# Attention units of two heads and one query tile, on both halves of TensorE's array, turned by transposes

## The chip, the cores and the metric

The kernel runs on one core of a Trainium2 chip. The metric is the device time of one execution in microseconds. Beside the runs that are timed there is one execution that the hardware profiler recorded; its rows are what is read here. The engines are TensorE (PE; its weight loads stand apart as PEld), VectorE (DVE), ScalarE (ACT), GpSimd (POOL) and SyncE (SP), which issues the weight DMAs. Engines run their own instruction lists in order and meet at semaphores.

## The reference, cut to what matters

Two transformer blocks, each of two layers, over 256 tokens of width 1024; everything is float32. Four attentions occur:

```python
# layer 0: 12 query heads of 64, 4 key/value heads; 256 context and 256 latent tokens
s = einsum('bkgqd,bksd->bkgqs', q, k) * 64 ** -0.5
p = softmax(s); o = einsum('bkgqs,bksd->bkgqd', p, v)
# context queries look at 256 keys, latent queries at 512
# layer 1: 6 heads with two 64-wide halves each, values 128 wide, 256 latent queries, 512 keys
p = softmax(einsum('bhiqd,bhisd->bhiqs', q, k) * 64 ** -0.5)
a = p[:, :, 0] - lam * p[:, :, 1]; o = einsum('bhqs,bhsd->bhqd', a, v)
# layers 2 and 3: cross attention, 4 heads of 64, 256 queries, 256 keys
```

Around them stand projections, normalizations, feed-forward layers (layers 0 and 1), an mLSTM (layer 2), an RG-LRU (layer 3), and an expert layer with 16384 experts (layers 2 and 3), which is most of the time.

## The kernel before, in words

The program is a list of stages (`STAGES`). Each engine runs its part of a stage after `enter`, which waits until the engines that take part in earlier stages have left them. So an attention stage (`attend0` to `attend3`) doesn't overlap the stage behind it: the stage behind begins when the last of TensorE, ScalarE and VectorE has left. SyncE is not in the stages: it streams all weights through a ring of 6 slots and is ahead as far as the ring lets it. No attention stage uses the ring; `attend0` also has GpSimd at `pool_windows` (22 us of its own), which attention doesn't wait for.

An attention stage is a row of units (`units_of`). In layers 0, 2 and 3 a unit is one head with two query tiles of 128 queries (`r` = 0, 1): 24 units in layer 0 (12 with 256 keys, then 12 with 512), 4 in each of layers 2 and 3 (256 keys). The head's 64 rows lie in the lower or the upper half of the partitions. In layer 1 a unit is one head with its two 64-wide halves and one query tile: 12 units of 512 keys ("diff" units).

What a unit takes, with the lines of the profile:

- TensorE `scores` (L822): two products, contraction over 64 rows, 128 queries by 256 or 512 keys, to two PSUM banks. Each float32 product is two MATMUL instructions.
- VectorE `maxima` (L1615, L1616): row maxima of both, times -1/8.
- ScalarE `exps` (L1344): two exponentials from PSUM to `probs`, each with its row sum.
- VectorE `diagonals` (L1622, L1626): reciprocals of the sums and two 128x128 diagonal matrices of them; in layer 1 the second times -lambda.
- TensorE `turn` (L838; L835 for diff units): product of each 128x128 piece of `probs` with its diagonal, which divides and turns it at once; for diff units the two halves add up in PSUM. To banks 4 and 5 (`pair`).
- VectorE `turned` (L1636): one copy of all of it to `probsT`.
- TensorE `heads` (L850): values (stationary, 64 columns; 128 in layer 1) with `probsT` (256 queries wide; 128 in layer 1), added over the key pieces.
- ScalarE `heads` (L1353): copy of the result to `mixed`.

The order is written out. TensorE: `scores(0)`, then for each i `scores(i+1)`, `heads(i-1)`, `turn(i)`. ScalarE: `exps(i+1)`, `heads(i-1)`. VectorE: `diagonals(i)`, `maxima(i+1)`, `turned(i)`, and in layer 3 `rglru_scans(i)` behind it. Scores, `probs` and `probsT` are double buffered, the turned banks are not.

Of the kernel before, what the change touches and what calls it, by code (L numbers as in the profile page):

```python
# [25 lines left out]
ALU = mybir.AluOpType  # L26
ACT = mybir.ActivationFunctionType
# [6 lines left out]
P = 128  # L34
D = 1024
T = 256
KD = D // P
DEPTH = 2
HD = 64
# [24 lines left out]
CTX, LAT = 0, 1  # L64
# [53 lines left out]
def stages_of(engine, before):  # L118
# [8 lines left out]


FEATURES, TOKENS = "features", "tokens"
PROJECT = {  # L130
    0: [(0, 8, 0, 2 * T, FEATURES, P), (8, 2, 0, 2 * T, TOKENS, P), (10, 2, 0, 2 * T, FEATURES, P)],
    1: [(18, 4, T, T, FEATURES, P), (0, 6, T, T, FEATURES, P), (6, 6, 0, 2 * T, FEATURES, P),
# [151 lines left out]
def program(nc, a, out):  # L284
    ctx = ExitStack()
    with ctx:
# [3 lines left out]
        def sem(name):  # L290
            return ctx.enter_context(nc.semaphore(name))
# [42 lines left out]
        def over(v, n):  # L334
# [18 lines left out]
        diag = part(WORK + 4096, 4, P)  # L353
# [52 lines left out]
        s_ready, m_ready, e_ready, d_ready, t_ready, pt_ready, o_ready, o_out = (sem(n) for n in (  # L406
            "scores_ready", "max_ready", "exp_ready", "diag_ready", "turned", "turned_out", "heads_ready", "heads_out"))
# [46 lines left out]
        def units_of(l):  # L454
            units = []
            if l == 0:
                for s in (CTX, LAT):
                    for n, head in enumerate(Q_ORDER):
                        j, half, kv = n // 2, n % 2, head // 3
                        assert half == kv % 2  # L460
                        rows = slice(half * HD, (half + 1) * HD)
                        units.append(dict(
                            nk=T if s == CTX else 2 * T, diff=False, rows=(half * HD, HD),
                            q=[proj[rows, j, s * T + r * P:s * T + (r + 1) * P] for r in range(2)],
                            k=[proj[rows, 6 + kv // 2, 0:T if s == CTX else 2 * T]] * 2,
                            v=lambda c, kv=kv: proj[:, 8 + kv // 2, c * P + (kv % 2) * HD:c * P + (kv % 2 + 1) * HD],
                            out=mixed[rows, j, s * T:(s + 1) * T]))
            elif l == 1:
                for h in range(6):
                    for t in range(2):  # L470
                        units.append(dict(
                            nk=2 * T, diff=True, rows=(0, P),
                            q=[proj[r * HD:(r + 1) * HD, h, t * P:(t + 1) * P] for r in range(2)],
                            k=[proj[r * HD:(r + 1) * HD, 6 + h, :] for r in range(2)],
                            v=lambda c, h=h: proj[:, 12 + h, c * P:(c + 1) * P],
                            out=mixed[:, h, t * P:(t + 1) * P]))
            else:
                for h in range(4):
                    j, half = h // 2, h % 2
                    rows = slice(half * HD, (half + 1) * HD)  # L480
                    units.append(dict(
                        nk=T, diff=False, rows=(half * HD, HD),
                        q=[proj[rows, 24 + j, r * P:(r + 1) * P] for r in range(2)],
                        k=[mem_k[rows, j, T:2 * T]] * 2,
                        v=lambda c, j=j, half=half: mem_v[:, j, T + c * P + half * HD:T + c * P + (half + 1) * HD],
                        out=mixed[rows, (6 if l == 2 else 8) + j, 0:T]))
# [147 lines left out]
        def _(pe):  # L634
# [176 lines left out]
            def attend(l):  # L811

                units = units_of(l)
                enter(pe, f"attend{l}")
                base = n_unit[0]

                def scores(i):
                    u = units[i]
                    if base + i >= 2:
                        pe.wait_ge(e_ready, base + i - 1)  # L820
                    for r in range(2):
                        last = mm(scores_at(i, u["nk"])[:, r, :], u["q"][r], u["k"][r], start=True, stop=True)  # L822
                    last.then_inc(s_ready, 1)

                def turn(i):
                    u = units[i]
                    pe.wait_ge(d_ready, base + i + 1)
                    if base + i:
                        pe.wait_ge(pt_ready, base + i)
                    for c in range(u["nk"] // P):  # L830
                        for r in range(2):
                            e = probs[:, i % 2, r, c * P:(c + 1) * P]
                            dg = diag[:, 2 * (i % 2) + r, :]
                            if u["diff"]:
                                last = mm(pair[:, 0, c * P:(c + 1) * P], e, dg, start=(r == 0), stop=(r == 1))  # L835
                            else:
                                at = (c % 2) * T + r * P
                                last = mm(pair[:, c // 2, at:at + P], e, dg, start=True, stop=True)  # L838
                    last.then_inc(t_ready, 1)

                def heads(i):
                    u = units[i]
                    pe.wait_ge(pt_ready, base + i + 1)
                    if base + i >= 2:
                        pe.wait_ge(o_out, base + i - 1)
                    nq = P if u["diff"] else 2 * P
                    lo, m = u["rows"]
                    chunks = u["nk"] // P
                    for c in range(chunks):
                        last = mm(single[lo:lo + m, i % 2, 0:nq], u["v"](c), probsT[:, i % 2, c * nq:(c + 1) * nq],  # L850
                                  start=(c == 0), stop=(c == chunks - 1))
# [12 lines left out]
                leave()  # L864
# [326 lines left out]
        def _(act):  # L1191
# [136 lines left out]
            def attend(l):  # L1328
# [9 lines left out]
                def exps(i):  # L1338
# [7 lines left out]
                                 accum_out=cols[:, 16 + b + r:17 + b + r])  # L1346
                    last.then_inc(e_ready, 1)

                def heads(i):
                    u = units[i]  # L1350
                    act.wait_ge(o_ready, base + i + 1)
                    lo, m = u["rows"]
                    f(u["out"], single[lo:lo + m, i % 2, 0:P if u["diff"] else 2 * P], ACT.Copy).then_inc(o_out, 1)  # L1353
# [163 lines left out]
        def _(dve):  # L1517
# [89 lines left out]
            def attend(l):  # L1607
# [8 lines left out]
                    v.tensor_scalar(cols[:, 8 + b:10 + b], cols[:, b:b + 2], -HD ** -0.5, None,  # L1616
                                    ALU.mult).then_inc(m_ready, 1)

                def diagonals(i):
                    b = 4 * (i % 2)  # L1620
                    dve.wait_ge(e_ready, base + i + 1)
                    chain(v.reciprocal(cols[:, 24 + b:26 + b], cols[:, 16 + b:18 + b]))  # L1622
                    for r in range(2):
                        second = neg_lam[:, 0:1] if units[i]["diff"] and r else None
                        op = (ALU.mult, ALU.mult) if second is not None else (ALU.mult,)
                        last = v.tensor_scalar(diag[:, 2 * (i % 2) + r, :], const("ident"),  # L1626
                                               cols[:, 24 + b + r:25 + b + r], second, *op)
                    last.then_inc(d_ready, 1)

                def turned(i):  # L1630
                    u = units[i]
                    dve.wait_ge(t_ready, base + i + 1)
                    if base + i >= 2:
                        dve.wait_ge(o_ready, base + i - 1)
                    n = u["nk"] * (1 if u["diff"] else 2)
                    v.tensor_copy(probsT[:, i % 2, 0:n], ps[:, 4:6, :].rearrange("p b n -> p (b n)")[:, 0:n])\  # L1636
                        .then_inc(pt_ready, 1)
# [12 lines left out]

# [625 lines left out]
```

## Time and profile before

| what | value |
|---|---|
| median of 3 runs | 3855.55 us (3855.47 to 3856.93) |
| the profiled execution | 3852.96 us, its span 3851.1 us |
| mean granted TensorE clock | 0.903 |
| PE busy | 91% of the span |
| stage attend0 (158.0 to 276.4) | 118.4 us |
| stage attend1 (948.2 to 1003.3) | 55.1 us |
| stage attend2 (1464.3 to 1492.0) | 27.7 us |
| stage attend3 (2698.5 to 2727.5) | 29.0 us |

The busy time of an engine counts what it ran; the row of a timeline gives start, duration, engine, line, operation, operands, the number of merged instructions, and in brackets how long the engine sat idle before and for whom. The granted clock is 1.0 where TensorE ran at 2.4 GHz and 0.5 where it ran at 1.2 GHz.

### The profile page before, as it was taken

To read this page: it belongs to the slowest core of one execution; us is meant where nothing else is said; L and a number is where in the kernel's file an instruction comes from. 1 tells how busy PE (TensorE), PEld (TensorE's weight loads), DVE (VectorE), ACT (ScalarE), POOL (GpSimd) and SP (SyncE) were. 2 spreads that over 40 slices of the span, in tenths; PEclk is the share of its full clock that TensorE was granted. 3 is DMA by queue.
4 is the path that set the end of the run, shared out by engine and by line. 5 is a ranking of instruction groups with operands and counts; after the bars stand their busy time and mean duration, and the time that the engine had idled before them with its cause. 6 is when DMAs were issued, how large, how long until landed. Compare 5 with 4: busy or idle time off the path is not lost.

```text
span 3851.1 us, 59762 instructions
## 1 busy us (share of the span) xinstructions
PE 3505.1 (91%) x21992; PEld 3056.0 (79%) x21992; DVE 2161.2 (56%) x3899; ACT 1226.0 (32%) x1840; POOL 93.5 (2%) x135
## 2 busy tenths in 40 slices
PE   7998998999889996679999999998758999999998
PEld 3567988967689765579999989986658899899997
DVE  2444545543455223866666666664396666666665
ACT  1223424421244212013444144443201444324444
POOL 0200000000000000200000000000020000000000
PEclk9999999999999987858999599999885899959999
DMA  7304545552145321203555045543120355504553
GB/s 268 135 10 172 185 169 186 185 197 88 44 148 185 127 77 44 88 0 118 187 185 186 21 158 185 186 160 120 60 77 0 136 185 186 188 2 174 186 187 128
DMA packets 140460, 512.94 MB, mean 133 GB/s; under 512 B 15904, under 2 KB 15904, under 8 KB 139584
## 3 DMA queue, kind: packets, MB, share of 16 engines
q1 hardware_dynamic: 139712, 507.48, 37.6%
q0 software_dynamic: 640, 4.00, 0.3%
q8 instruction: 71, 1.16, 0.1%
q14 instruction: 37, 0.30, 0.0%
HBM read 510.37 MB, written 1.05 MB: 133 GB/s over the span
## 4 chain that ended last, share of the span: by engine, by line
PE 85%; DVE 9%; ACT 2%; issue 1%; DMA 1%; PEld 1%; DVEq 0%; ACTq 0%; POOL 0%; PEldq 0%; SPq 0%; POOLq 0%
PE ps L878 29%; PE ps L936 22%; PE ps L1119 10%; PE ps L869 4%; PE ps L755 4%; PE ps L713 3%; PE ps L758 1%; PE ps L850 1%; PE ps L822 1%; PE ps L838 1%; PE ps L1081 1%; PE ps L907 1%; PE ps L901 1%; DVE arena L1530 1%; PE ps L718 1%
## 5 line engine op out<-in xcount | busy, mean ns | idle before, releaser
L1728 DVE TENSOR_TENSOR w_split<-ring,w_split 128x1024 fp32r<-128x1024 f32 x710 | 869.3, 1226 | 689.5 <-ACT w_split L1405 666.2
L878 PEld LDWEIGHTS ps<-x_split,w_split 128*128 128x128 f32 x9312 | 1170.5, 194 | 72.9 <-issue 48.0
L878 PE MATMUL ps<-x_split,w_split 128*128 128x256 f32 x9312 | 1179.7, 285 | 46.1 <-DVE w_split L1728 46.1
L1405 ACT ACTIVATE w_split<-ring 128x1024 fp32r<-128x1024 f32 x710 | 751.0, 1060 | 1126.8 <-PE ps L878 677.3
L936 PE MATMUL ps<-w_split,h_split 128*128 128x512 f32 x3864 | 934.3, 391 | 0.0
L936 PEld LDWEIGHTS ps<-w_split,h_split 128*128 128x128 f32 x3864 | 706.0, 188 | 133.7
L1119 PE MATMUL ps<-arena 128*128 128x64 bf16 x3072 | 373.6, 302 | 16.3 <-DVE arena L2019 16.3
L1119 PEld LDWEIGHTS ps<-arena 128*128 128x128 bf16 x3072 | 372.7, 146 | 17.6 <-issue 17.6
L1436 ACT ACTIVATE arena<-ps 128x512 f32 x128 | 77.1, 602 | 328.2 <-PE ps L1119 328.2
L1749 DVE TENSOR_TENSOR x<-x,arena 128x256 f32<-128x256 f32 x256 | 158.3, 618 | 16.6 <-ACT x L1411 16.6
L869 PE MATMUL ps<-arena,ring 128*128 128x256 f32 (+1 forms) x672 | 150.1, 386 | 9.2 <-DVEq L1524 7.1
L755 PE MATMUL ps<-arena,ring 128*128 128x512 f32 (+1 forms) x416 | 153.2, 522 | 4.8 <-ACTq L1197 4.8
L869 PEld LDWEIGHTS ps<-arena,ring 128*128 128x128 f32 (+1 forms) x672 | 130.1, 194 | 29.8 <-issue 10.7
L713 PE MATMUL ps<-x,ring 128*128 128x256 f32 (+1 forms) x608 | 133.6, 382 | 6.3 <-ACTq L1197 6.3
L1081 PE MATMUL ps<-x,ring 128*128 128x256 f32 x512 | 122.3, 395 | 18.7 <-DVEq L1524 18.7
L755 PEld LDWEIGHTS ps<-arena,ring 128*128 128x128 f32 x416 | 80.5, 195 | 67.7 <-issue 62.6
L713 PEld LDWEIGHTS ps<-x,ring 128*128 128x128 f32 (+1 forms) x608 | 109.2, 180 | 30.1 <-issue 7.1
L2015 DVE TENSOR_TENSOR arena<-arena 128x512 bf16<-128x512 bf16 x128 | 54.5, 425 | 134.4 <-PE ps L1119 124.7
L1081 PEld LDWEIGHTS ps<-x,ring 128*128 128x128 f32 x512 | 99.7, 200 | 33.0 <-issue 19.4
L1530 DVE RECIPROCAL arena<-arena 128x256 f32<-128x256 f32 (+2 forms) x26 | 63.1, 2429 | 107.1 <-ACT arena L1308 107.1
L2019 DVE TENSOR_TENSOR arena<-arena 128x1536 bf16<-128x1536 bf16 x128 | 121.8, 952 | 0.0
L1739 DVE TENSOR_TENSOR h_split<-x,h_split 128x256 fp32r<-128x256 f32 x256 | 109.1, 426 | 8.7
(258 smaller groups left out, 2423.6 us busy)
## 6 DMA issues: line engine op xcount, KB each, us to landing
ring<-in_peer_u SPq DMA_DIRECT2D x256, 512.0 KB, 3.2
ring<-in_peer_v SPq DMA_DIRECT2D x256, 512.0 KB, 3.2
ring<-in_ffn_in SPq DMA_DIRECT2D x132, 512.0 KB, 3.2
ring<-in_ada SPq DMA_DIRECT2D x96, 512.0 KB, 4.5
ring<-in_ffn_out SPq DMA_DIRECT2D x66, 512.0 KB, 3.2
ring<-in_pq SPq DMA_DIRECT2D x32, 512.0 KB, 3.2
ring<-in_ml_in SPq DMA_DIRECT2D x26, 512.0 KB, 3.2
ring<-in_cd_in SPq DMA_DIRECT2D x22, 512.0 KB, 3.4
```

The costliest lines, as they stand in the source:

```text
L713: last = mm(pair[0:width, par, 0:nt], w[:, k, :], src[:, k, t0:t0 + nt], start=(k == 0), stop=(k == KD - 1))
L755: last = mm(pair[:, n % 2, 0:nt], w[:, k, :], hT[:, k, t0:t0 + nt], start=(k == 0), stop=(k == KD - 1))
L869: last = mm(wide[:, m, :], ring[0:rows, blk[0], m * P:(m + 1) * P], rhs, start=(first and m % 2 == 0), stop=final, skip_group_check=True)
L878: last = mm(dst, w_split[:, w, wp, at:at + P], rhs[rp], start=(first and i == 0), stop=(final and i == 2), skip_group_check=shared)
L936: last = mm(ps[:, 2 * r + c, :], h_split[:, ph, hp, r * P:(r + 1) * P], w_split[:, b[3], wp, c * 512:(c + 1) * 512], start=(first and i == ...
L1081: last = mm(pair[:, m % 2, 0:T], ring[:, b[0], k * P:(k + 1) * P], x[:, LAT, k, :], start=(k == 0), stop=(k == KD - 1))
L1119: last = mm(single[:, b, u * HALF:(u + 1) * HALF], hot_i[:, b, :, u], hot_w[:, b, c, :, u], start=(c == 0), stop=(c == 2))
L1405: f(w_split[:, w, 0, :], ring[:, slot, :], ACT.Copy).then_inc(w_high, 1)
L1728: v.tensor_tensor(w_split[:, w, 1, :], ring[:, slot, :], w_split[:, w, 0, :].bitcast(F32), ALU.subtract).then_inc(w_low, 1)
L1739: v.tensor_tensor(h_split[:, ph, 1, :], raw[:, ph, :], h_split[:, ph, 0, :].bitcast(F32), ALU.subtract).then_inc(hid_ready, 1)
L1749: return v.tensor_tensor(coef[:, ph, :], gelu[:, ph, :], g, ALU.mult)
L2019: v.tensor_tensor(hot_w[:, b], hot_j[:, b].unsqueeze(1).to_broadcast([P, 3, HALF, GROUP]), weight3[:, :, at].unsqueeze(2).to_broadcast([P, ...
```

## The change

Units of layers 0, 2 and 3 become two heads (the lower and upper half of the partitions) with one query tile; their number stays the same. The diagonals go: VectorE's `divided` scales `probs` in place, and `turn` becomes one transpose for each 128x128 piece. For diff units `divided` forms p1/s1 - lambda p2/s2 first, so half as many pieces are turned. The copy of the turned pieces is parted: VectorE the first head, ScalarE the second; ScalarE alone for diff units. VectorE's order becomes `maxima(i+1)`, `divided(i)`, `turned(i-1)`; ScalarE's `exps(i+1)`, `turned(i-1)`, `heads(i-2)`. TensorE's order stays `scores(i+1)`, `heads(i-1)`, `turn(i)`.

```diff
+HALVES = [slice(0, HD), slice(HD, P)]
...
-                    for n, head in enumerate(Q_ORDER):
...
+                    for j in range(6):
+                        kv = Q_ORDER[2 * j] // 3 // 2
...
+                        for r in range(2):
+                            at = s * T + r * P
+                            units.append(dict(
+                                nk=nk, diff=False, q=[proj[rows, j, at:at + P] for rows in HALVES],
+                                k=[proj[rows, 6 + kv, 0:nk] for rows in HALVES],
+                                v=lambda c, half, kv=kv: proj[:, 8 + kv, c * P + half * HD:c * P + (half + 1) * HD],
+                                out=mixed[:, j, at:at + P]))
...
                 def turn(i):
                     u = units[i]
                     pe.wait_ge(d_ready, base + i + 1)
                     if base + i:
-                        pe.wait_ge(pt_ready, base + i)
-                    for c in range(u["nk"] // P):
-                        for r in range(2):
-                            e = probs[:, i % 2, r, c * P:(c + 1) * P]
-                            dg = diag[:, 2 * (i % 2) + r, :]
...
+                        pe.wait_ge(pt_second, base + i)
+                    if not u["diff"] and firsts + i:
+                        pe.wait_ge(pt_first, firsts + i)
+                    for half in range(1 if u["diff"] else 2):
+                        for c in range(u["nk"] // P):
+                            last = nc.tensor.transpose(pair[:, half, c * P:(c + 1) * P],
+                                                       probs[:, i % 2, half, c * P:(c + 1) * P], const("ident"))
                     last.then_inc(t_ready, 1)
                 def heads(i):
                     u = units[i]
-                    pe.wait_ge(pt_ready, base + i + 1)
+                    pe.wait_ge(pt_second, base + i + 1)
+                    if not u["diff"]:
+                        pe.wait_ge(pt_first, firsts + i + 1)
...
                     for c in range(chunks):
+                        for half in range(1 if u["diff"] else 2):
+                            rows = slice(0, P) if u["diff"] else HALVES[half]
+                            last = mm(single[rows, i % 2, 0:P], u["v"](c, half),
+                                      probsT[:, i % 2, half * 512 + c * P:half * 512 + (c + 1) * P],
+                                      start=(c == 0), stop=(c == chunks - 1))
...
+                def turned(i):
+                    u = units[i]
+                    act.wait_ge(t_ready, base + i + 1)
+                    if base + i >= 2:
+                        act.wait_ge(o_ready, base + i - 1)
+                    half = 0 if u["diff"] else 1
+                    f(probsT[:, i % 2, half * 512:half * 512 + u["nk"]], pair[:, half, 0:u["nk"]], ACT.Copy)\
+                        .then_inc(pt_second, 1)
...
                 exps(0)
                 for i in range(n):
                     if i + 1 < n:
                         exps(i + 1)
                     if i:
-                        heads(i - 1)
+                        turned(i - 1)
+                    if i >= 2:
+                        heads(i - 2)
+                turned(n - 1)
+                heads(n - 2)
                 heads(n - 1)
...
-                def diagonals(i):
+                def divided(i):
                     b = 4 * (i % 2)
                     dve.wait_ge(e_ready, base + i + 1)
                     chain(v.reciprocal(cols[:, 24 + b:26 + b], cols[:, 16 + b:18 + b]))
...
+                    one, two = (probs[:, i % 2, half, 0:units[i]["nk"]] for half in range(2))
+                    if units[i]["diff"]:
+                        v.tensor_scalar(cols[:, 26 + b:27 + b], cols[:, 25 + b:26 + b], neg_lam[:, 0:1], None, ALU.mult)
+                        chain(v.tensor_scalar(one, one, cols[:, 24 + b:25 + b], None, ALU.mult))
+                        last = v.scalar_tensor_tensor(one, two, cols[:, 26 + b:27 + b], one, ALU.mult, ALU.add)
+                    else:
+                        v.tensor_scalar(one, one, cols[:, 24 + b:25 + b], None, ALU.mult)
+                        last = v.tensor_scalar(two, two, cols[:, 25 + b:26 + b], None, ALU.mult)
                     last.then_inc(d_ready, 1)
...
                 maxima(0)
                 for i in range(n):
-                    diagonals(i)
                     if i + 1 < n:
                         maxima(i + 1)
-                    turned(i)
+                    divided(i)
+                    if i and not units[i - 1]["diff"]:
+                        turned(i - 1)
                     if l == 3:
                         rglru_scans(i)
+                if not units[n - 1]["diff"]:
+                    turned(n - 1)
```

## Rows read from the trace of the kernel before

**Rows 1.** The page's chain that ended last, shares of the span by engine.
```profile
PE 85%; DVE 9%; ACT 2%; issue 1%; DMA 1%; PEld 1%; DVEq 0%; ACTq 0%; POOL 0%; PEldq 0%; SPq 0%; POOLq 0%
```

**Rows 2.** Stretches: length, busy PE, PEld, DVE, ACT, POOL; granted clock, DMA share, GB/s.
```profile
158.00:276.40 118.40, 110.29 (x528) 69.78 (x528) 65.74 (x144) 38.77 (x121) 21.83 (x21) 0.96 0.02 5
948.20:1003.30 55.10, 49.06 (x336) 38.48 (x336) 31.49 (x72) 23.26 (x64) 0.00 (x0) 0.97 0.03 11
1464.30:1492.00 27.70, 21.03 (x64) 13.46 (x64) 8.43 (x24) 6.83 (x21) 0.00 (x0) 0.53 0.00 0
2698.50:2727.50 29.00, 18.98 (x64) 12.09 (x64) 17.47 (x34) 6.76 (x21) 0.00 (x0) 0.65 0.00 1
...
1018.00:1022.00 4.00, 2.47 (x6) 2.05 (x7) 2.47 (x3) 0.00 (x0) 0.00 (x0) 0.50 0.02 4
1022.00:1026.00 4.00, 4.00 (x19) 3.49 (x18) 0.00 (x0) 0.00 (x0) 0.00 (x0) 0.94 0.10 18
```

**Rows 3.** Timeline (start, duration, then what), attend0, units of 256 keys.
```profile
163.93 2.08 PE L838 MATMUL ps<-arena 128*128 128x128 f32 x8 [4.80 <-DVE arena L1626]
...
184.09 0.47 ACT L1344 ACTIVATE arena<-ps,cols 128x256 f32<-128x256 f32 x1 [1.34 <-DVE cols L1616]
...
185.00 0.37 ACT L1353 ACTIVATE arena<-ps 64x256 f32<-64x256 f32 x1
```

**Rows 4.** Timeline, attend0, units of 512 keys.
```profile
202.80 1.23 DVE L1615 TENSOR_REDUCE cols<-ps 128x2 f32<-128x1024 f32 x1 [0.63 <-PE ps L822]
...
204.26 0.69 ACT L1344 ACTIVATE arena<-ps,cols 128x512 f32<-128x512 f32 x1 [2.98 <-DVE cols L1616]
...
205.60 0.37 ACT L1353 ACTIVATE arena<-ps 64x256 f32<-64x256 f32 x1
...
215.45 1.98 PE L822 MATMUL ps<-arena 64*128 64x512 f32 x4
...
217.36 1.94 PE L850 MATMUL ps<-arena 128*64 128x256 f32 x8
...
219.23 2.05 PE L838 MATMUL ps<-arena 128*128 128x128 f32 x16
...
221.21 1.98 PE L822 MATMUL ps<-arena 64*128 64x512 f32 x4
```

**Rows 5.** Timeline, attend1, the first two diff units.
```profile
948.22 1.99 PE L822 MATMUL ps<-arena 64*128 64x512 f32 x8 [0.77 <-ACTq L1197]
...
949.49 1.23 DVE L1615 TENSOR_REDUCE cols<-ps 128x2 f32<-128x1024 f32 x1 [12.26 <-PE ps L822]
...
954.28 3.63 PE L835 MATMUL ps<-arena 128*128 128x128 f32 x16 [4.07 <-DVE arena L1626]
```

**Rows 6.** Timeline, attend2, first units, the clock at 0.5.
```profile
1471.03 2.08 PE L838 MATMUL ps<-arena 128*128 128x128 f32 x8 [4.55 <-DVE arena L1626]
...
1473.04 2.07 PE L822 MATMUL ps<-arena 64*128 64x256 f32 x4
...
1475.15 0.69 DVE L1615 TENSOR_REDUCE cols<-ps 128x2 f32<-128x512 f32 x1 [0.72 <-PE ps L822]
...
1476.08 0.47 ACT L1344 ACTIVATE arena<-ps,cols 128x256 f32<-128x256 f32 x1 [3.24 <-DVE cols L1616]
```

**Rows 7.** Timeline of TensorE: transposes behind a hidden stage; products on four 32-column groups.
```profile
521.39 1.97 PE L965 MATMUL ps<-consts,arena 128*128 128x128 f32 x16 [0.69 <-ACT arena L1426]
...
89.72 1.50 PE L652 MATMUL ps<-ring,cond_wide 128*32 128x256 f32 x24
```

**Rows 8.** Groups by line (busy us, mean ns of one): copies, a scaling; and a scan pair in attend3.
```profile
L1436 ACT ACTIVATE arena<-ps 128x512 f32 x128 | 77.1, 602 | 328.2 <-PE ps L1119 328.2
L1411 ACT ACTIVATE x<-ps 128x256 f32<-128x256 f32 x256 | 94.3, 368 | 20.9 <-PE ps L878 20.9
L1668 DVE TENSOR_SCALAR res<-x 128x2048 f32<-128x2048 f32 x6 | 7.3, 1224 | 1.7 <-ACTq L1197 1.1 <-DVEq L1524 0.6
...
2709.93 1.27 DVE L1904 TENSOR_TENSOR_SCAN arena<-arena 96x256 f32<-96x256 f32 x2
```

More of the change, by code:

```diff
@@ L352, in program @@
         probsT = part(WORK + 2048, 2, 1024)
-        diag = part(WORK + 4096, 4, P)
         h2 = part(0, KD, T)
@@ L405, in program @@
             "squared", "mean_ready", "normed", "partner_ready", "roped"))
-        s_ready, m_ready, e_ready, d_ready, t_ready, pt_ready, o_ready, o_out = (sem(n) for n in (
-            "scores_ready", "max_ready", "exp_ready", "diag_ready", "turned", "turned_out", "heads_ready", "heads_out"))
+        s_ready, m_ready, e_ready, d_ready, t_ready, pt_first, pt_second, o_ready, o_out = (sem(n) for n in (
+            "scores_ready", "max_ready", "exp_ready", "divided", "turned", "first_head_kept", "second_head_kept", "heads_ready",
+            "heads_out"))
         sum_ready = sem("sum_ready")
@@ L457, in units_of @@
                 for s in (CTX, LAT):
-                    for n, head in enumerate(Q_ORDER):
[L459 to L467, printed above, removed]
+                    nk = T if s == CTX else 2 * T
@@ new lines, in units_of @@
+                    for j in range(6):
+                        kv = Q_ORDER[2 * j] // 3 // 2
+                        assert [Q_ORDER[2 * j + half] // 3 for half in range(2)] == [2 * kv, 2 * kv + 1]
+                        for r in range(2):
[5 more added lines that the diff above has]
+                                out=mixed[:, j, at:at + P]))
@@ L468, in units_of @@
             elif l == 1:
                 for h in range(6):
-                    for t in range(2):
+                    for r in range(2):
                         units.append(dict(
[L472 to L476, printed above, removed]
-            else:
[L478 to L486, printed above, removed]
@@ L487, in units_of @@
-            return units
+                            nk=2 * T, diff=True, q=[proj[rows, h, r * P:(r + 1) * P] for rows in HALVES],
+                            k=[proj[rows, 6 + h, :] for rows in HALVES],
+                            v=lambda c, half, h=h: proj[:, 12 + h, c * P:(c + 1) * P],
+                            out=mixed[:, h, r * P:(r + 1) * P]))
+            else:
+                for j in range(2):
+                    for r in range(2):
+                        units.append(dict(
+                            nk=T, diff=False, q=[proj[rows, 24 + j, r * P:(r + 1) * P] for rows in HALVES],
+                            k=[mem_k[rows, j, T:2 * T] for rows in HALVES],
+                            v=lambda c, half, j=j: mem_v[:, j, T + c * P + half * HD:T + c * P + (half + 1) * HD],
+                            out=mixed[:, (6 if l == 2 else 8) + j, r * P:(r + 1) * P]))
@@ L489, in scores_at, with first_heads @@
+            return units
+        def first_heads(l):
+            return 24 if l == 1 else sum(len(units_of(m)) for m in range(l) if m != 1)
         def scores_at(i, nk):
@@ L814, in attend @@
                 enter(pe, f"attend{l}")
-                base = n_unit[0]
+                base, firsts = n_unit[0], first_heads(l)
                 def scores(i):
@@ L828, in turn @@
                     if base + i:
-                        pe.wait_ge(pt_ready, base + i)
-                    for c in range(u["nk"] // P):
-                        for r in range(2):
-                            e = probs[:, i % 2, r, c * P:(c + 1) * P]
-                            dg = diag[:, 2 * (i % 2) + r, :]
[L834 to L838, printed above, removed]
+                        pe.wait_ge(pt_second, base + i)
[5 more added lines that the diff above has]
+                                                       probs[:, i % 2, half, c * P:(c + 1) * P], const("ident"))
                     last.then_inc(t_ready, 1)
@@ L842, in heads @@
                     u = units[i]
-                    pe.wait_ge(pt_ready, base + i + 1)
+                    pe.wait_ge(pt_second, base + i + 1)
+                    if not u["diff"]:
+                        pe.wait_ge(pt_first, firsts + i + 1)
                     if base + i >= 2:
                         pe.wait_ge(o_out, base + i - 1)
-                    nq = P if u["diff"] else 2 * P
-                    lo, m = u["rows"]
                     chunks = u["nk"] // P
                     for c in range(chunks):
-                        last = mm(single[lo:lo + m, i % 2, 0:nq], u["v"](c), probsT[:, i % 2, c * nq:(c + 1) * nq],
-                                  start=(c == 0), stop=(c == chunks - 1))
+                        for half in range(1 if u["diff"] else 2):
[3 more added lines that the diff above has]
+                                      start=(c == 0), stop=(c == chunks - 1))
                     last.then_inc(o_ready, 1)
@@ L1347, in exps @@
                     last.then_inc(e_ready, 1)
+                def turned(i):
[6 more added lines that the diff above has]
+                        .then_inc(pt_second, 1)
                 def heads(i):
-                    u = units[i]
                     act.wait_ge(o_ready, base + i + 1)
-                    lo, m = u["rows"]
-                    f(u["out"], single[lo:lo + m, i % 2, 0:P if u["diff"] else 2 * P], ACT.Copy).then_inc(o_out, 1)
+                    f(units[i]["out"], single[:, i % 2, 0:P], ACT.Copy).then_inc(o_out, 1)
                 n = len(units)
@@ L1622, in diagonals @@
                     chain(v.reciprocal(cols[:, 24 + b:26 + b], cols[:, 16 + b:18 + b]))
[L1623 to L1627, printed above, removed]
+                    one, two = (probs[:, i % 2, half, 0:units[i]["nk"]] for half in range(2))
[6 more added lines that the diff above has]
+                        last = v.tensor_scalar(two, two, cols[:, 25 + b:26 + b], None, ALU.mult)
                     last.then_inc(d_ready, 1)
@@ L1634, in turned @@
                         dve.wait_ge(o_ready, base + i - 1)
-                    n = u["nk"] * (1 if u["diff"] else 2)
-                    v.tensor_copy(probsT[:, i % 2, 0:n], ps[:, 4:6, :].rearrange("p b n -> p (b n)")[:, 0:n])\
-                        .then_inc(pt_ready, 1)
+                    v.tensor_copy(probsT[:, i % 2, 0:u["nk"]], pair[:, 0, 0:u["nk"]]).then_inc(pt_first, 1)
                 n = len(units)
```

## The prediction

> **What bounds the kernel now.** I read the chain of waits first: the reader sees TensorE's products on 85% of it [rows 1], so what counts is how long TensorE is kept. Then the stretches of the four attention stages [rows 2]: together 118.4 + 55.1 + 27.7 + 29.0 = 230.2 us, 6% of the span, and nothing of another stage beside them, so a change of their length goes into the total in full. Then the timeline inside a stage. In a unit of 512 keys TensorE goes from scores (215.45) to heads (217.36) to turn (219.23) to the next scores (221.21) and has no idle time in brackets: 5.76 us a unit, all TensorE [rows 4]. The stretches say the same: PE busy 110.3 of 118.4 and 49.1 of 55.1. The order before lets VectorE and ScalarE work beside that. So before, these stages are bound by TensorE, at a granted clock of 0.96 and 0.97; attend2 and attend3 ran mostly at 1.2 GHz (0.53 and 0.65) [rows 2].
>
> **What the new order makes of it.** TensorE's list at step i is still scores(i+1), heads(i-1), turn(i). heads(i-1) now waits for ScalarE's copy of unit i-1, and that copy stands in ScalarE's list behind exps(i+1), which waits for VectorE's maxima(i+1), which wait for scores(i+1), issued by TensorE just before. So the whole step is one ring: scores(i+1), maxima(i+1), exps(i+1), copy(i-1), heads(i-1), turn(i), and only then scores(i+2). Nothing in it lies beside anything else. VectorE's own branch is shorter: after maxima(i+1) it has divided(i) and the copy of the first head. A scaling of 2048 columns takes 1.22 us [rows 8], so 512 take some 0.3; two of them with the reciprocal 0.9, the copy of 512 columns some 0.7, together 1.6 us, against exps and copy on ScalarE, 1.9 us. For diff units the second pass has two inputs; even at 0.7 us the diff division ends at 1.7 and has no copy behind it. This branch costs nothing; if it were 0.5 us longer, 0.2 us a step would show.
>
> **The terms of a step**, at 2.4 GHz first:
> - Scores. In layer 1 the two products already lie on both halves, and the timeline shows them side by side: 8 instructions of 512 columns in 1.99 us, where 4 of one half take 1.98 [rows 4, 5]. From their start to the start of the maxima: 1.27 us for 512 keys [rows 5]; for 256 keys half of the streaming goes (0.43), 0.84. At 1.2 GHz 4 serial instructions of 256 columns take 1473.04 to 1475.15, 2.11 us; two pairs side by side of 512 columns stream as long, 2.11, and of 256 columns 0.85 less, 1.26 [rows 6].
> - Maxima until exps start: 202.80 to 204.26, 1.46 us for 512 keys [rows 4]; 1475.15 to 1476.08, 0.93 for 256 [rows 6].
> - Both exps until ScalarE's next operation: 204.26 to 205.60, 1.34 [rows 4]; 184.09 to 185.00, 0.91 [rows 3].
> - Copy by ScalarE: 0.60 for 512 columns, 0.37 for 256 [rows 8], and 0.06 to hand on (the maxima start 0.04 behind the products' end, rows 6).
> - Heads. New are column halves side by side. The nearest row has four 32-column groups: 24 instructions of 256 columns in 1.50 us, six groups of four, so one group each (1.50 - 0.38)/5 = 0.22 us, as if it were one instruction [rows 7]. With 128 columns that is 0.11 for a pair: 4 pairs for 256 keys, 8 for 512, 8 full instructions in a diff unit. With 0.15 for the change of the tile: 0.59, 1.03, 0.9. At 1.2 GHz 1.04, 1.9, 1.8.
> - Turn. 16 transposes take 1.97 us, (1.97 - 0.27)/15 = 0.11 each, one instruction each [rows 7], where a product with a diagonal needs two (16 in 2.05 for 8 pieces, rows 4). So 4, 8, and 4 (diff) transposes and 0.2 until the next scores: 0.64, 1.07, 0.64; at 1.2 GHz 1.1, 1.96, 1.1.
>
> The Trainium skill, "TensorE: Matmul & The Clock Gate", section "Terms", says that the transpose mode is four times faster for FP32; the row shows twice against two-instruction diagonal products. By that rule the turns would be half as long again, and the sum below some 20 us smaller.
>
> Sums of a step at 2.4 GHz: 256 keys 0.84 + 0.93 + 0.91 + 0.43 + 0.59 + 0.64 = 4.3 us; 512 keys 1.27 + 1.46 + 1.34 + 0.66 + 1.03 + 1.07 = 6.8; diff 1.27 + 1.46 + 1.34 + 0.66 + 0.9 + 0.64 = 6.3. At 1.2 GHz: 1.26 + 0.93 + 0.91 + 0.43 + 1.04 + 1.1 = 5.7; 2.11 + 1.46 + 1.34 + 0.66 + 1.9 + 1.96 = 9.4; diff 2.11 + 1.46 + 1.34 + 0.66 + 1.8 + 1.1 = 8.5.
>
> **Which clock.** In both large stages TensorE waits 4.8 and 4.1 us for the first exps and then starts its turn at 1.2 GHz: 8 instructions in 2.08 us, 16 in 3.63 [rows 3, 5]. Before, it was then packed without a gap and came back to 2.4 GHz. In attend2 it was busy 21.0 of 27.7 us and stayed at 0.53 [rows 2]. In the new ring it works 3.2 of 5.7, 6.0 of 9.4, 5.0 of 8.5 us at the low level, less densely than in that stretch. I take it that the clock stays at 1.2 GHz through all four stages; that is my choice, and the other end is a rival. Of the transposes, the Trainium skill says ("TensorE: Matmul & The Clock Gate", Part 4) that they don't count as activity for the gate; no row here shows that, and it would only make the low level surer.
>
> **The sum.** attend0: the first turn starts at 163.9 [rows 3], with divided on 256 columns in place of 128 at 164.1, and ends its step at 165.2. Ten steps of 5.7 to 222.4; two mixed ones of 7.5 and 8.4 to 238.3; ten of 9.4 to 332.3; the last (no scores or exps left: copy, heads, turn, copy, heads, output) 0.75 + 1.9 + 1.96 + 0.75 + 1.9 + 0.5 = 7.8, to 340.1. Before 276.4: +63.7. attend1: first turn at 954.3 [rows 5] plus 0.9 for the longer division, its step ends 956.3; ten steps of 8.5 to 1041.3, end 6.7, 1048.0; before 1003.3: +44.7. attend2: first turn 1471.1, step ends 1472.2 [rows 6], two steps of 5.7 to 1483.6, end 4.8, 1488.4; before 1492.0: -3.6. attend3 the same shape, but after divided(0) VectorE has its scans before maxima(2) (a pair 1.27 us [rows 8]), and in the last step they stand ahead of its last copy: -2. Behind attend0, attend2 and attend3 a dense product stage now starts at 1.2 GHz. Such a start is seen behind attend1: 0.50 until 1022, 0.94 in the next 4 us [rows 2], TensorE starting at 1019.5; half of 2.7 us is lost: 3 x 1.4 = +4. Bounds 0 and 10 for the three. SyncE, the ring and the DMAs take nothing: no weights are used in these stages. Sum: 63.7 + 44.7 - 3.6 - 2 + 4 = +107 us on the profiled execution's 3853.0: 3960. The median of the runs stands 2.6 above that execution, so 3962.
>
> Unknown terms: column halves (below: none of the other direction; above: weight loads one after the other, a rival), the hand-on (0 to 0.2 us in 5 places of 36 steps: -10 to +20).
>
> **Rivals.**
> 1. The clock returns to 2.4 GHz, or does so for part of the stages. For: before, it came back in both large stages (0.96 and 0.97 over all), and the change makes the array fuller in scores and heads. Against: the gaps above. All of it: attend0 165.2 + 5.7 + 9 x 4.3 + 5.8 + 6.2 + 10 x 6.8 + 4.9 = 294.5 (+18), attend1 956.3 + 10 x 6.3 + 4.8 = 1024.1 (+21), the small stages -5.6: +34, 3889. In part: 3889 to 3940.
> 2. The ring isn't closed: ScalarE's copy gets by without the new exps, and the engines overlap. Then each step is its busiest engine: TensorE some 3.1 us for 512 keys (0.85 + 0.2 + 1.03 + 1.07) against 5.76, 2.0 against 3.15 for 256 keys (VectorE: 0.69 + 0.2 + 0.2 + 0.4 + 0.4), 2.9 against 3.93 for diff units (VectorE): 12 x (2.66 + 1.15 + 1.0) = -58, with the small stages -6: 3792, faster. It decides only if TensorE reaches heads(i-1) without waiting for exps(i+1). For it speaks that TensorE's own work falls by 40%; against it the two written orders.
> 3. The change doesn't do what it says in the heads: the loads of the two column halves come one after the other. Then 4 or 8 more loads a step at up to 0.23 us (1.2 GHz): +0.8 and +1.8 us, 11 x 0.8 + 12 x 1.8 = +30: 3992. Against: the four-group row.
>
> **Chances.** Forecast 0.73 (its own range 3940 to 3985); rival 1 0.17; rival 2 0.04; rival 3 0.05; a result within 0.2% (8 us, about what a measurement of this kernel tells from no change) 0.01. The range 3888 to 3988 reaches from rival 1 at its full size nearly to rival 3. Faster 0.04, same 0.01, slower 0.95.
>
> **What would show it.** In the profile after: a steady unit of 512 keys with scores, maxima, exps, ScalarE's copy, heads, turn one after another and TensorE idle before heads with ScalarE's copy as releaser, about 3.5 us; steps of 5.7, 9.4, 8.5 us; a granted clock near 0.5 in attend0 and attend1; transposes of 0.11 us (0.22 at the low level); the scans of attend3 unchanged. A step shorter than 5.76 us for 512 keys, or TensorE idle for VectorE instead, makes the ring wrong; steps near 6.8 make the clock wrong.

## Result, and the profile after

| | time, us |
|---|---|
| before | 3856.24 median (3855.47 to 3857.29, 4 runs) |
| after | 3942.39 median (3938.67 to 3946.68, 4 runs) |
| ratio | 1.0223, 95% interval 1.021 to 1.0236: slower |
| forecast | 3962 (3888 to 3988) |
| profiled execution after | 3946.68, span 3944.9, clock 0.88 |

The four attention stages after, as stretches (length, busy PE, PEld, DVE, ACT, POOL, granted clock, DMA share, GB/s); they answer to [rows 2]:

```profile
158.80:333.70 174.90, 98.59 (x529) 62.81 (x529) 63.63 (x144) 44.29 (x145) 21.51 (x21) 0.65 0.01 4
1004.90:1101.50 96.60, 54.78 (x192) 35.82 (x192) 33.91 (x73) 29.11 (x76) 0.00 (x0) 0.62 0.02 6
1561.60:1584.60 23.00, 13.17 (x65) 8.16 (x65) 7.79 (x24) 7.36 (x25) 0.00 (x0) 0.50 0.00 0
2794.30:2819.40 25.10, 13.17 (x65) 8.14 (x65) 16.76 (x34) 7.35 (x25) 0.00 (x0) 0.50 0.00 0
```

The stages took 118.4, 55.1, 27.7 and 29.0 us before and 174.9, 96.6, 23.0 and 25.1 after: +56.5, +41.5, -4.7, -3.9, together +89.4 of the 93.8 us by which the profiled spans differ. PE is busy 98.6 of 174.9 us where it was busy 110.3 of 118.4, and the clock went from 0.96 and 0.97 to 0.65 and 0.62.

One whole step of 512 keys with the clock high throughout, from the timeline of the changed kernel; it answers to [rows 4]. L825 are the scores, L1629 the maxima, L1347 the exps, L1636 starts the division, L1652 and L1358 are VectorE's and ScalarE's copies of the turned pieces, L852 is heads, L837 the turn:

```profile
294.25 1.13 PE L825 MATMUL ps<-arena 64*128 64x512 f32 x4
295.43 1.23 DVE L1629 TENSOR_REDUCE cols<-ps 128x2 f32<-128x1024 f32 x1 [5.00 <-PE ps L825]
...
296.76 0.16 DVE L1636 RECIPROCAL cols<-cols 128x2 f32<-128x2 f32 x1
296.89 0.69 ACT L1347 ACTIVATE arena<-ps,cols 128x512 f32<-128x512 f32 x1 [5.92 <-DVE cols L1630]
...
297.75 0.69 DVE L1652 COPY arena<-ps 128x512 f32<-128x512 f32 x1
298.23 0.59 ACT L1358 ACTIVATE arena<-ps 128x512 f32<-128x512 f32 x1
...
298.88 1.09 PE L852 MATMUL ps<-arena 128*64 128x128 f32 x16 [3.50 <-ACT arena L1358]
299.90 1.09 PE L837 MATMUL ps<-consts,arena 128*128 128x128 f32 x8
300.93 1.13 PE L825 MATMUL ps<-arena 64*128 64x512 f32 x4
```

These rows show the ring. From the scores it is 1.18 us to the maxima, 1.46 to the exps, 1.34 to ScalarE's copy, 0.65 to heads (TensorE idle for 3.50 us, ended by that copy), 1.02 to the turn and 1.03 to the next scores: 6.68 us. VectorE's copy ended at 298.44, 0.4 us before ScalarE's. All other full steps of 512 keys were longer, 8.42 to 9.12 us, with the clock low in part of them. A step of 256 keys, all at 1.2 GHz, answers to [rows 6]:

```profile
192.93 1.23 PE L825 MATMUL ps<-arena 64*128 64x256 f32 x4
194.21 0.69 DVE L1629 TENSOR_REDUCE cols<-ps 128x2 f32<-128x512 f32 x1 [3.70 <-PE ps L825]
...
195.14 0.47 ACT L1347 ACTIVATE arena<-ps,cols 128x256 f32<-128x256 f32 x1 [4.18 <-DVE cols L1630]
...
196.05 0.38 ACT L1358 ACTIVATE arena<-ps 128x256 f32<-128x256 f32 x1
...
196.49 1.12 PE L852 MATMUL ps<-arena 128*64 128x128 f32 x8 [2.33 <-ACT arena L1358]
197.54 1.12 PE L837 MATMUL ps<-consts,arena 128*128 128x128 f32 x4
198.59 1.22 PE L825 MATMUL ps<-arena 64*128 64x256 f32 x4
```

The waits of heads over the whole execution (who for whom, total us, times, longest), in the kernel before and then in the changed one:

```profile
PE ps L850 <- DVE arena L1636: 7.3, 8, 1.3
...
PE ps L852 <- ACT arena L1358: 110.2, 41, 3.5
```

### The profile page after: what moved, and what is told of

It is laid out like the page before. It is cut to its first block, busy times and chain, and to the rows that moved or that the text cites. A ratio compares the mean times of both kernels' runs of the same rounds, so it can differ in the third digit from the quotient of the medians.

```text
span 3944.9 us, 59550 instructions
## 1 busy us (share of the span) xinstructions
PE 3489.8 (88%) x21848; PEld 3041.3 (77%) x21848; DVE 2160.1 (55%) x3899; ACT 1238.6 (31%) x1884; POOL 93.1 (2%) x135
## 3 DMA queue, kind: packets, MB, share of 16 engines
HBM read 510.37 MB, written 1.05 MB: 130 GB/s over the span
## 4 chain that ended last, share of the span: by engine, by line
PE 83%; DVE 9%; ACT 3%; issue 1%; DMA 1%; PEld 1%; DVEq 0%; ACTq 0%; POOL 0%; PEldq 0%; SPq 0%; POOLq 0%
PE ps L881 28%; PE ps L939 22%; PE ps L1122 9%; PE ps L872 4%; PE ps L758 4%; PE ps L716 3%; PE ps L852 2%; PE ps L761 1%; PE ps L825 1%; PE ps L837 1%; DVE cols L1629 1%; PE ps L1084 1%; PE ps L910 1%; PE ps L904 1%; ACT arena L1347 1%
## 5 line engine op out<-in xcount | busy, mean ns | idle before, releaser
L852 PEld LDWEIGHTS ps<-arena 128*64 128x64 f32 (+1 forms) x448 | 53.4, 237 | 159.7 <-ACT arena L1358 152.9
L852 PE MATMUL ps<-arena 128*64 128x128 f32 (+1 forms) x448 | 69.2, 421 | 120.0 <-ACT arena L1358 110.2
L1629 DVE TENSOR_REDUCE cols<-ps 128x2 f32<-128x1024 f32 (+1 forms) x44 | 43.4, 986 | 175.0 <-PE ps L825 175.0
```

The costliest lines, as they stand in the source:

```text
L852: last = mm(single[rows, i % 2, 0:P], u["v"](c, half), probsT[:, i % 2, half * 512 + c * P:half * 512 + (c + 1) * P], start=(c == 0), stop ...
L1629: chain(v.tensor_reduce(cols[:, b:b + 2], scores_at(i, units[i]["nk"]), AX_X, ALU.max))
```

## Experiments

All edits are to the changed kernel. Times are medians of 4 runs; the kernel before had 3853.8 us in the first batch (copy-first, ScalarE only, filled, shape only) and 3857.5 in the second (VectorE only, best of both, products, first wait only). Ratios are to the kernel before in the same batch. Stage lengths are stretches of the profiled execution, from the stage's first instruction to the first of the next stage.

**1. Copies first, on both engines.**

```diff
 # ScalarE
-                    if i + 1 < n:
-                        exps(i + 1)
                     if i:
                         turned(i - 1)
+                    if i + 1 < n:
+                        exps(i + 1)
 # VectorE
-                    if i + 1 < n:
-                        maxima(i + 1)
-                    divided(i)
                     if i and not units[i - 1]["diff"]:
                         turned(i - 1)
+                    divided(i)
+                    if i + 1 < n:
+                        maxima(i + 1)
```

> The changed kernel with two order edits: ScalarE copies unit i-1 before the exps of unit i+1; VectorE does the copy of unit i-1, then divided(i), then maxima(i+1). Theory 1 (the closed ring: heads(i-1) waits for work that starts only with scores(i+1)) expects that TensorE reaches heads(i-1) straight behind scores(i+1), and that a step becomes VectorE's chain maxima, exps, division: 512 keys 1.46 + 1.34 + 1.1 = about 4.0 us in place of 6.7 to 9.4, 256 keys about 2.8 in place of 5.65, diff units 1.46 + 1.34 + 1.5 = about 4.3; attend0 some 90 to 100 us in place of 175, attend1 56 to 62 in place of 96; total 3820 to 3845, faster than the kernel before. Theory 2 (the cost lies in the new work itself, transposes, in-place divisions, or in the clock alone) expects at most 10 us of change against 3942.

Measured 3815.72 us, ratio 0.9899 (0.9883 to 0.9916), 4 us below the expected range. attend0 93.5 us, attend1 58.6, both in theirs. Timeline, 512 keys:

```profile
221.38 1.13 PE L825 MATMUL ps<-arena 64*128 64x512 f32 x4
221.48 0.69 DVE L1652 COPY arena<-ps 128x512 f32<-128x512 f32 x1 [0.41 <-PE ps L837]
...
222.59 0.17 DVE L1636 RECIPROCAL cols<-cols 128x2 f32<-128x2 f32 x1 [0.41 <-ACT arena L1347]
222.60 0.60 ACT L1358 ACTIVATE arena<-ps 128x512 f32<-128x512 f32 x1
...
223.26 1.09 PE L852 MATMUL ps<-arena 128*64 128x128 f32 x16 [0.75 <-ACT arena L1358]
223.58 1.22 DVE L1629 TENSOR_REDUCE cols<-ps 128x2 f32<-128x1024 f32 x1
...
225.04 0.69 ACT L1347 ACTIVATE arena<-ps,cols 128x512 f32<-128x512 f32 x1 [1.83 <-DVE cols L1630]
...
225.31 1.13 PE L825 MATMUL ps<-arena 64*128 64x512 f32 x4
```

The step is 3.93 us, and it is the chain through VectorE and ScalarE: maxima to exps 1.46, exps to division 1.48, division to the next maxima 0.99. VectorE's other wait, 0.41 us for the turn, lies beside the exps and costs nothing. The instructions are the same and only their order differs, and the kernel is 127 us faster than the changed one: theory 1 holds, theory 2 falls. The clock rose with it (0.87 and 0.88 in the two large stages), so a part of the 127 us is the clock's; experiment 4 takes the two apart.

**2. ScalarE's copy first alone** (the first hunk of 1).

> The changed kernel with one order edit: ScalarE copies unit i-1 before the exps of unit i+1; VectorE keeps maxima(i+1), divided(i), copy of the first head. Theory 1 (two branches close the ring, ScalarE's was only the later by about 0.3 us) expects that attention with two heads in a unit hardly gains, because the ring closes through VectorE: 512 keys 1.27 + 1.3 + 1.15 + 0.7 + 1.03 + 1.07 = 6.5 us at 2.4 GHz against 6.7, 256 keys about 0.3 us less a step; but diff units, whose only copy is ScalarE's, fall to scores, maxima, division, turn = 1.27 + 1.4 + 1.5 + 0.64 = 4.8 us at 2.4 GHz. attend0 160 to 175 us (175 before), attend1 62 to 72 (96 before), total 3900 to 3925. A theory in which only ScalarE's copy holds TensorE up expects attend0 near 100 too and a total below 3850.

Measured 3909.38 us, ratio 1.0139 (1.0122 to 1.0156), as theory 1 expects. attend0 171.4 us, attend1 67.6 us; 256-key steps 5.41 in place of 5.65, diff steps 4.74 where the clock was high. Timeline, 512 keys:

```profile
305.52 0.60 ACT L1358 ACTIVATE arena<-ps 128x512 f32<-128x512 f32 x1 [3.95 <-PE ps L837]
...
309.87 0.68 DVE L1652 COPY arena<-ps 128x512 f32<-128x512 f32 x1
...
310.65 1.70 PE L852 MATMUL ps<-arena 128*64 128x128 f32 x16 [3.16 <-issue]
```

ScalarE's copy now ends 4.5 us before heads, and heads still starts 0.10 behind the end of VectorE's copy (310.55), after 3.16 us idle in place of 3.50. The row names no releaser ("issue"); that it was this copy is read from the order of the ends. The second branch closes the ring 0.3 us shorter. Diff units have no copy on VectorE and are freed: nearly all of the 33 us gained are in attend1.

**3. VectorE's copy first alone** (the second hunk of 1).

> The changed kernel with the other half of the order edit alone: VectorE does the copy of unit i-1, divided(i), maxima(i+1); ScalarE keeps exps(i+1) ahead of its copy. Theory 1 (the ring closes through ScalarE's copy as long as that stands behind exps(i+1)) expects a step as long as in the changed kernel or longer, by what VectorE does ahead of the maxima where that ends after the scores: 256 keys: copy 0.4 and division 0.7 start when turn(i-1) is done and end 0.2 to 0.4 us behind a score pair at either clock; 512 keys: copy 0.7 and division 1.15 end 0.6 us behind it at 2.4 GHz and before it at 1.2; diff units 1.45, 0.2 us at 2.4 GHz. attend0 174 to 182 us, attend1 95 to 100, total 3938 to 3955. A theory in which either order edit alone frees TensorE expects attend0 below 150.

Measured 3950.25 us, ratio 1.0238 (1.0221 to 1.0255), as theory 1 expects; attend0 178.9, attend1 95.7. Timeline, 512 keys:

```profile
295.05 0.69 DVE L1652 COPY arena<-ps 128x512 f32<-128x512 f32 x1 [5.63 <-PE ps L837]
...
299.44 0.59 ACT L1358 ACTIVATE arena<-ps 128x512 f32<-128x512 f32 x1
...
300.09 1.97 PE L852 MATMUL ps<-arena 128*64 128x128 f32 x16 [4.02 <-ACT arena L1358]
```

VectorE's copy now ends 4.3 us before heads, and ScalarE's copy ends the wait. In units of two heads either edit alone leaves the ring; both together open it.

**4. TensorE kept busy with products that nobody reads.**

```diff
                     if i + 1 < n:
                         scores(i + 1)
+                    if i + 1 < n:
+                        if base + i >= 3:
+                            pe.wait_ge(o_out, base + i - 2)
+                        for _ in range(9 if i == 0 else 3 if units[i + 1]["nk"] == T else 6):
+                            mm(single[:, (i + 1) % 2, T:2 * T], const("ident"), const("cos"), start=True, stop=True)
                     if i:
                         heads(i - 1)
```

> The changed kernel with products added on TensorE that nobody reads (identity by a 128x256 constant, to columns that are not used): 9 behind scores(1), 3 in a unit of 256 keys, 6 in one of 512 keys, in each step where TensorE is idle before heads(i-1) (2.3 and 3.5 us). They tell the price of the clock. The theory that TensorE's gaps let the clock fall, and that a step's TensorE parts then take twice as long, expects a granted clock near 1.0 in all stages and steps of 4.4, 6.7 and 6.3 us: attend0 135 to 142 us, attend1 74 to 78, the small stages 18 to 20, total 3870 to 3890. If the clock has another cause, the clock stays and the added products (0.43 us each at 2.4 GHz, 0.85 at 1.2) lengthen the steps: total over 3945.

Measured 3878.94 us, ratio to before 1.006 (1.0044 to 1.0077). Its two large stages as stretches:

```profile
158.90:296.80 137.90, 114.68 (x750) 79.13 (x751) 64.64 (x144) 44.29 (x145) 21.54 (x21) 0.99 0.01 5
966.70:1040.30 73.60, 63.89 (x330) 45.40 (x330) 33.92 (x72) 29.12 (x76) 0.00 (x0) 1.00 0.02 8
```

With more work on TensorE the kernel is 63.5 us faster than the changed one: steps 4.20, 6.67 and 6.15 us (256 keys, 512 keys, diff). The total and attend0 are in the expected ranges; attend1 (73.6) is just below its own, and the two small stages (20.1 and 22.4 us) are above the 18 to 20 expected. So of the change's +86 us the new kernel at the high clock is +25 (3878.9 against 3853.8; the gain of the new shape, experiment 5, is in it), and the low clock is the other 63. The two do not add up to 86 exactly because the kernel before was 2.4 us faster in this batch than in the first result.

**5. The new shape of the units alone.** Diagonals, products with them, VectorE's single copy, and the order before:

```diff
 # TensorE, turn
+                    for c in range(u["nk"] // P):
+                        for half in range(2):
+                            e = probs[:, i % 2, half, c * P:(c + 1) * P]
+                            dg = diag[:, 2 * (i % 2) + half, :]
...
 # VectorE
-                    if i + 1 < n:
-                        maxima(i + 1)
-                    divided(i)
...
+                    diagonals(i)
+                    if i + 1 < n:
+                        maxima(i + 1)
+                    turned(i)
```

> Only the new shape of the units: two heads on the two halves of the array with one query tile. Diagonals, products with them, one copy by VectorE and the old order as in the kernel before. The theory that the new shape is a gain that the new order hides expects scores 0.43 or 0.85 us shorter and heads as much shorter: a step of 4.2 us for 512 keys (5.76 before), 2.6 for 256 keys (3.15), diff units unchanged at 3.93; attend0 92 to 98 us, total 3825 to 3838. The rival that the column halves don't run side by side or bring a stall when the tile changes expects attend0 at 118 us or more and a total of 3850 to 3865.

Measured 3827.79 us, ratio 0.9924 (0.9908 to 0.9941), in the expected range. Timeline, 512 keys:

```profile
226.20 1.13 PE L826 MATMUL ps<-arena 64*128 64x512 f32 x4
...
227.58 1.09 PE L853 MATMUL ps<-arena 128*64 128x128 f32 x16 [0.26 <-DVE arena L1638]
228.61 2.05 PE L841 MATMUL ps<-arena 128*128 128x128 f32 x16
...
230.59 1.13 PE L826 MATMUL ps<-arena 64*128 64x512 f32 x4
```

A step takes 4.39 us in place of 5.76: scores 1.13 for 1.98, heads 1.09 for 1.94, since both halves of the array work at once. attend0 95.9 us, attend1 56.5 (55.1 before, at a clock of 0.94 for 0.97). The shape is a gain by itself.

**6. Best of both:** copies first for units of two heads; for diff units diagonals, products with them and the old order.

> The copy-first orders for the units of two heads, and for diff units (layer 1) what the kernel before has: diagonals, products with them, one copy by VectorE, its order. Theory (each unit form at its own better bound: 3.93 us a step both for 512 keys by maxima, exps, division and for diff units by the old order) expects attend0 93.5 us as with copy-first, attend1 55 to 57 in place of 58.6, total 2 to 4 us below copy-first alone, 3808 to 3818; a rival is that the gain is lost to where the clock falls, and the total is the same within 2 us.

Measured 3813.03 us, ratio 0.988 (0.9863 to 0.9896), the lowest median of all; attend0 95.3, attend1 55.0. attend1 gained 3.6 us, as expected; attend0, which should have stayed, lost 1.8: its clock was 0.85 for 0.87, falling once more at 249.2, near the stage's end, where that of copy-first stayed high. The interval overlaps that of copy-first (0.9883 to 0.9916), so whether it is faster stays open.

**7. Plain products with the identity in place of transposes.**

```diff
-                            last = nc.tensor.transpose(pair[:, half, c * P:(c + 1) * P],
-                                                       probs[:, i % 2, half, c * P:(c + 1) * P], const("ident"))
+                            last = mm(pair[:, half, c * P:(c + 1) * P], probs[:, i % 2, half, c * P:(c + 1) * P],
+                                      const("ident"), start=True, stop=True)
```

> The changed kernel with each transpose replaced by a plain float32 product with the identity (two instructions of 0.11 us at 2.4 GHz in place of one). Tells whether transposes weigh less for the clock than products. If they weigh the same, the longer turns (0.44 us for 256 keys and diff, 0.88 for 512 keys at 2.4 GHz, twice that at 1.2) fill TensorE a little more and the clock of attend0 rises from 0.65 to 0.7 at most; steps grow, total 3950 to 3970. If transposes don't count, the products are new activity in every step: granted clock 0.8 or more in both large stages, and a total of 3920 to 3945.

Measured 3983.91 us, ratio 1.0326 (1.0308 to 1.0343), above both expectations.

```profile
159.30:362.60 203.30, 128.24 (x672) 97.36 (x673) 62.42 (x144) 44.29 (x145) 21.49 (x21) 0.61 0.01 3
1033.50:1136.30 102.80, 61.14 (x240) 45.42 (x240) 33.91 (x72) 29.12 (x76) 0.00 (x0) 0.68 0.02 5
```

The granted clock is 0.61 and 0.68 where the transposes had 0.65 and 0.62: far from the 0.8 expected if transposes counted for nothing, and on the whole no sign that a product holds the clock better. The expected rise to 0.7 in attend0 did not come either. The turn itself took 3.7 us for 8 pieces at the low clock against 1.9, and 2.0 against 1.05 for 4. The transposes were a saving inside the ring.

**8. Filling only the first wait** of each stage, on top of 6: 9 unread products behind scores(1).

> The best version so far (copy-first orders, diff units as before) with 9 products that nobody reads behind scores(1) of each attention stage, where TensorE waits 4 to 5 us for the first exps. If the low clock at the start of each stage is owed to this wait alone, the clock is 0.95 or more in all four stages and they are together 8 to 12 us shorter: attend0 86 to 90 us, total 3800 to 3812. If the steps that follow are too thin to hold the clock, it falls anyway and the total is the same as without them within 3 us.

Measured 3815.95 us, ratio 0.989 (0.9873 to 0.9906); version 6 had 3813.03. In attend1 the clock stayed at 1.0 and the stage took 53.6 us, 1.4 less, which is within the noise of the total. In attend0 the filling moved the fall of the clock from 163.9 to 167.2; it was then low for 20.5 us in place of 23.9, and the stage took 95.5 (clock 0.87). So the first wait alone isn't what costs attend0 its clock. That the 256-key steps are too thin to hold it, the other theory, is not shown and stands against this trace: from 188.7 on, steps of 2.7 us with TensorE busy for 1.88 of them ran at 1.0 throughout. The clock fell inside a wait of 1.34 us before heads, behind one of 1.81 us before the first turn, beside GpSimd's work; what let it fall is open.

## Why the prediction was right, and where it was off

- The bound before, the ring after, and its order were right: the wait of heads for ScalarE's copy, 3.50 us, is the "about 3.5 us" forecast, and experiments 1 to 3 show the ring as the cause and both its branches. The VectorE branch was said to end about 0.3 us earlier; experiment 2 gives 0.3. (A scaling of 512 columns took 0.49 us for the 0.3 forecast, but from the end of the maxima to the end of the copy it was 1.68 for 1.6.)
- The sums of a step, forecast and measured: 256 keys at 1.2 GHz 5.7 and 5.65, at 2.4 GHz 4.3 and 4.20; 512 keys at 2.4 GHz 6.8 and 6.68; diff at 1.2 GHz 8.5 and 8.44, at 2.4 GHz 6.3 and 6.15 (4.20 and 6.15 are of experiment 4). No step of 512 keys ran wholly at 1.2 GHz, so the 9.4 stays untested. Transposes of 0.11 us and column halves side by side: right. (Where the prediction says of the turns "half as long again", the 20 us that it takes off the sum belong to half as long.) Rival 3 (loads of the halves one after the other) fell: 16 heads instructions in 1.09 us.
- The step that failed is "I take it that the clock stays at 1.2 GHz through all four stages". It did in all full steps of 256 keys and in both small stages. In the 512-key and diff units it came back for short stretches (0.65 and 0.62 over the two stages, where the prediction named "near 0.5" as its sign), and the steps were 8.4 to 9.1 (one 6.68) in place of 9.4 and 7.5 to 8.4 in place of 8.5. So the low clock's term was too large: attend0 +56.5 against +63.7, attend1 +41.5 against +44.7. The row of attend2 that it rested on is of 256-key units, whose forecast held; it was carried over to fuller units. Rival 1 in part (the clock returns for part of the stages, 3889 to 3940) is the mechanism that the trace shows, and its edge is 2 us from the median of 3942, the forecast 20.
- The sum left one cost out. It took "nothing of another stage beside them", but GpSimd's `pool_windows` runs beside the start of attend0, and there the new in-place divisions ran slowly. The first turn came 7.1 us behind the stage's start in place of 6.1, and two steps took 7.38 and 7.31 us in place of 5.65: +4.4 us together. In these two steps VectorE's branch, said to cost nothing, ended the wait of heads. One division beside GpSimd with that wait, and half of a division later, from the timeline:

```profile
169.61 0.80 DVE L1643 TENSOR_SCALAR arena<-arena,cols 128x256 f32<-128x256 f32 x1
...
170.33 1.42 DVE L1644 TENSOR_SCALAR arena<-arena,cols 128x256 f32<-128x256 f32 x1
...
172.23 1.12 PE L852 MATMUL ps<-arena 128*64 128x128 f32 x8 [4.07 <-DVE arena L1652]
...
195.21 0.35 DVE L1643 TENSOR_SCALAR arena<-arena,cols 128x256 f32<-128x256 f32 x1
```

- That the median fell into the forecast's own range (3940 to 3985) is in part luck: the low clock's term was too large and GpSimd's was missing, and the two errors partly cancel. Up to the end of the ten 256-key steps attend0 took 68.0 us for the 64.4 forecast, and from there 106.9 for 117.7. Without the 4.4 us beside GpSimd the kernel would stand near 3938, an estimate from these rows, in the range of rival 1 in part. Of the 20 us between forecast and median, 13 are the sum's (93.8 for 107 between the profiled executions), and 7 come from setting the median 2.6 us above the profiled execution, where it lay 4.3 below.
- attend2 and attend3: forecast -3.6 and -2, measured -4.7 and -3.9. The forecast kept the first turn where it was; it came 5.66 and 5.65 us behind the first scores for 6.64 and 6.33 before, the first unit's two products now lying side by side (attend2's first maxima start 1.36 us behind the scores for 2.18). The dense starts behind them began at the low clock, as forecast: behind attend2 the first 128 products took 29.27 us for 27.86, the 1.4 us forecast; behind attend3 the clock of the first 4 us was 0.55 for 1.00, some 1.8 us by that. Behind attend0 it cost none, since its end was at the high clock. The whole stretches behind attend2 and attend3 grew by 3.2 and 1.9 us; what the rest of the 3.2 is stays open, and the stretches behind attend0 and attend1 shrank by 0.6 and 0.9.
- Rival 2 (engines overlap, 3792) is what experiment 1 built by changing the order, and it reached 3816. The rival had left out the chain maxima, exps, division, which bounds a step at 3.93 us where the busiest engine alone would allow 3.1.

## What to carry to other kernels

When each engine is put one step behind its producer, write down for one step who waits for whom and in which list position: if the copy that frees the oldest unit stands behind the work on the newest one, the pipeline is a ring and each step is the sum of the parts of all engines. Put the operation that finishes old work ahead of the one that starts new work, and on every engine that has a branch of the ring: where there were two branches (attend0, 174.9 us), one alone gave 3.5 us or cost 4.0, both together gave 81. And an edit that lightens the engine that was the bound can lower its clock: price the steps at both levels before calling the lighter engine a gain.

## What the runs showed of the hardware

- The granted clock alternated inside a steady loop: in the 512-key units of the changed kernel single steps of 8.43, 8.67, 6.68, 8.42 and 8.76 us follow one another with mean clocks of 0.67, 0.73, 1.0, 0.68 and 0.72. It rose while heads, turn and scores stood packed (at 293.8 and 310.8) and fell in the wait before heads (at 304.0 and 314.2); the wait before the heads of 298.88, 3.50 us like the others, did not lower it. From 164.0 to 228.9, over the 256-key units, it was low for 64.9 us without a break. Products without use made the kernel 63.5 us faster.
- A float32 transpose of 128x128 takes one instruction and 0.11 us where a product of that size takes two: the turn of 8 pieces took 1.09 us (transposes) and 2.05 (experiment 5, products with diagonals) at 2.4 GHz.
- A VectorE scaling of 128x256 in place takes 0.35 us alone and 0.59 to 1.42 while GpSimd runs tensor operations; an exp of the same size on ScalarE took 0.47 in both. That VectorE and GpSimd share something is a guess; no run here took GpSimd away.
